# Two decoder layers on one Trainium2 core: the sums of squares of the norms taken for four tiles together in four column groups, and three merge blocks that go through their columns in interleaved runs

## The reference

```
h = rmsnorm(x, g_pre);  proj = h @ w_in
y = mixers(proj)                      # layer 1: S5, short convolution, attention; layer 2: four others
merged = sum_b sigmoid(gate_b) * (y_b @ w_branch_b)     # three branches in layer 1, four in layer 2
x = x + rmsnorm(merged @ w_out, g_post)
x = x + rmsnorm(mlp(rmsnorm(x, g_pre_mlp)), g_post_mlp)
rmsnorm(x, g) = x * rsqrt(mean(x*x over the 1024 channels) + 1e-6) * g
```

## Time and profile before

| | |
|---|---|
| median of three executions | 3498.69 us |
| the profiled execution's own time | 3496.17 us |
| its span, first to last instruction | 3494.5 us (1.7 us lie around it) |
| TensorE busy with matmuls | 3397.4 us, 97% of the span |
| DVE, ScalarE, GpSimd busy | 1357.1, 946.0, 909.0 us |
| mean granted TensorE clock | 0.995 |

### The profile page before, as it was taken

One profiled execution on the slowest core, in us unless ns is written; L12 is line 12 of the kernel. 1 busy time (PEld: TensorE's weight loads), 2 busy tenths in 40 slices (PEclk: granted clock), 3 DMA queues, 4 the chain that ended last, 5 costly groups with the idle time before them and its releaser, 6 DMA issues. The chain is left out here.

```text
span 3494.5 us, 40873 instructions
## 1 busy us (share of the span) xinstructions
PE 3397.4 (97%) x16184; PEld 2791.9 (80%) x16184; DVE 1357.1 (39%) x1651; ACT 946.0 (27%) x1248; POOL 909.0 (26%) x450
## 2 busy tenths in 40 slices
PE   8999999999999999999999999999999999999997
PEld 6788888887877888888868887777778688888886
DVE  6843556444325121212153336554552521121123
ACT  3222434344323111111133333313342411111112
POOL 2211111112341222222422114231254222222225
PEclk9999999999999999999999999999999999999998
DMA  3535434215422111111224323223353211111113
GB/s 128 157 94 157 151 121 151 85 61 211 141 76 79 48 48 48 48 48 48 97 102 132 95 73 127 79 73 141 132 195 124 79 48 48 48 48 48 48 49 131
DMA packets 101602, 333.42 MB, mean 95 GB/s; under 512 B 11920, under 2 KB 21520, under 8 KB 101328
## 3 DMA queue, kind: packets, MB, share of 16 engines
q1 hardware_dynamic: 100432, 327.95, 28.0%
q10 hardware_dynamic: 1040, 3.67, 0.3%
HBM read 249.06 MB, written 85.52 MB: 96 GB/s over the span
## 5 line engine op out<-in xcount | busy, mean ns | idle before, releaser
L282 POOL TENSOR_TENSOR w_lo<-w_raw,w_hi 128x1024 fp32r<-128x1024 f32 (+1 forms) x304 | 698.2, 2301 | 2423.8 <-ACT w_hi L278 2423.7
L322 PE MATMUL pair<-act_hi,w_hi 128*128 128x512 f32 x2976 | 942.8, 398 | 6.6 <-DVE f1v L1957 1.5
L322 PE MATMUL pair<-act_lo,w_hi 128*128 128x512 f32 x2976 | 920.5, 391 | 0.0
L322 PE MATMUL pair<-act_hi,w_lo 128*128 128x512 f32 x2976 | 918.8, 390 | 0.0
L322 PEld LDWEIGHTS pair<-act_hi,w_lo 128*128 128x128 f32 x2976 | 559.3, 188 | 119.6
L322 PEld LDWEIGHTS pair<-act_lo,w_hi 128*128 128x128 f32 x2976 | 559.5, 188 | 119.4
L322 PEld LDWEIGHTS pair<-act_hi,w_hi 128*128 128x128 f32 x2976 | 540.3, 189 | 111.2 <-issue 9.0
L278 ACT CAST w_hi<-w_raw 128x1024 fp32r<-128x1024 f32 x274 | 287.6, 1050 | 866.5 <-PE pair L322 820.7
L609 DVE TENSOR_TENSOR p<-pair,rs 128x1024 f32<-128x1024 f32 x100 | 122.2, 1222 | 402.8 <-PE pair L322 402.7
L1900 DVE TENSOR_TENSOR f2v<-pair,rs 128x1024 f32<-128x1024 f32 x42 | 51.4, 1225 | 333.1 <-PE pair L322 333.1
L322 PE MATMUL pair<-f1hh,w_hi 128*128 128x512 f32 x480 | 147.8, 389 | 0.0
(11 more groups left out here) (478 smaller groups left out, 4065.2 us busy)
## 6 DMA issues: line engine op xcount, KB each, us to landing
w_raw<-in_stream SPq DMA_DIRECT2D x275, 512.0 KB, 3.5
proj<-p SPq DMA_DIRECT2D x101, 512.0 KB, 2.6
m2g<-proj SPq DMA_DIRECT2D x32, 512.0 KB, 4.8
m1g<-proj SPq DMA_DIRECT2D x16, 512.0 KB, 3.4
x<-f1y SPq DMA_DIRECT2D x16, 512.0 KB, 2.6
act_lo<-x SPq DMA_DIRECT2D x16, 512.0 KB, 6.6
foxx<-proj SPq DMA_DIRECT2D x28, 256.0 KB, 5.8
fx_cb<-fox_cum SPq DMA_DIRECT2D x8, 512.0 KB, 7.3
```

The costliest lines, as they stand in the source:

```text
L282: last = nc.gpsimd.tensor_tensor(wlo[:, slot, at:at + n], raw[:, slot, at:at + n], whi[:, slot, at:at + n].bitcast(F32), ALU.subtract)
L322: last = nc.tensor.matmul(out_pair[:, h * HALF:(h + 1) * HALF], wt, a[:, h * HALF:(h + 1) * HALF], start=k == 0 and n_pass == 0, stop=k == ...
```

## The change

In `bridge`, the square of tile k goes to buffer k % 4 of the half row buffers of `late.x`. TensorE no longer sums each square. At k = 3 and k = 7 it waits for the last of four squares and issues four matmuls, each with 32 columns of ones and each into its own 32 partitions of the bank; so group n of partitions holds the sums of tiles n and n + 4. The squares of tiles 4 to 7 wait for the sum at k = 3. Then ScalarE copies the bank to `rs` (`partial`), and `half_sums` of that copy gives, per token on the partitions, 32 times the total; DVE's `half_root` is called without `rows`, so that L472 and L474 go and only the small scale-and-add stays, now after step (1, 1) for half 0. The copy of half 0 stands in ScalarE's queue ahead of everything of half 1; the sum of half 1's copy stands on TensorE ahead of `head.tile(1, 1, 3)`. DVE's first eviction now also waits for the last sum of squares, since the squares lie in `late.x`.

In `products`, blocks 9, 13 and 17 of the first merge address their columns in another order: the 512 columns of a half are taken as two rows of 256, and runs of 32, 64 or 16 columns are taken from the two rows in turn, for the moving operand and for the output alike. The values and where they land are the same.

```diff
@@ -295,7 +295,11 @@
         split_unit(0, 0, 1)
         fetch_unit(2, 0)
-    def products(i, base, per_turn, n_out, tiles, rhs, evict, ahead=False):
+    def in_runs(x, c):
+
+        return x.rearrange("p (a b c) -> p b a c", a=2, c=c) if c else x
+
+    def products(i, base, per_turn, n_out, tiles, rhs, evict, ahead=False, runs=None):
@@ -319,7 +323,8 @@
                 w_hi, w_lo = (x[:, slot, w * P:(w + 1) * P] for x in (whi, wlo))
                 for n_pass, (wt, a) in enumerate(((w_hi, hi), (w_hi, lo), (w_lo, hi))):
                     for h in range(2):
-                        last = nc.tensor.matmul(out_pair[:, h * HALF:(h + 1) * HALF], wt, a[:, h * HALF:(h + 1) * HALF],
+                        half, c = slice(h * HALF, (h + 1) * HALF), runs[o] if runs and o in runs else None
+                        last = nc.tensor.matmul(in_runs(out_pair[:, half], c), wt, in_runs(a[:, half], c),
                                                 start=k == 0 and n_pass == 0, stop=k == tiles - 1 and n_pass == 2)
                 if w == 7 or (not packed and k == tiles - 1):
                     last.then_inc(s_mm, 1)
@@ -331,13 +336,13 @@
                 yield
             evict(i, o, out_pair, ready, reads.mark)
-    def stage(turns, per_turn, n_out, tiles, rhs, evict, per=None, ahead=False):
+    def stage(turns, per_turn, n_out, tiles, rhs, evict, per=None, ahead=False, runs=None):
         if ahead:
             b = used["units"] + 1
             split_unit(b, b % 2, b // 2 + 1)
         if turns == 1:
-            for _ in products(0, used["units"], per_turn, n_out, tiles, rhs, evict):
+            for _ in products(0, used["units"], per_turn, n_out, tiles, rhs, evict, False, runs):
                 pass
         else:
             assert per_turn % 2 == 0 and n_out % 2 == 0
@@ -545,14 +550,16 @@
             split[h, k] = V.mark(V.after(a).scalar_tensor_tensor(act_lo[:, k, half], yk, g,
                                                                  act_hi[:, k, half].bitcast(F32),
                                                                  ALU.mult, ALU.subtract))
-            free = (done[h][k - 2],) if k > 1 else (done[0][-1], summed) if h else ()
-            a = A.mark(A.after(*free).activation(sq(h, k % 2), yk, ACT.Square))
+            a = A.mark(A.after(done[h][-1] if k > 3 else done[0][-1] if h else None).activation(sq(k % 4), yk, ACT.Square))
             PE.after(split[h, k])
             head.tile(0, h, k)
             if k >= lag[h]:
                 head.tile(1, h, k - lag[h])
-            PE.after(a)
-            done[h].append(PE.mark(nc.tensor.matmul(sides[h], ones[:], sq(h, k % 2), start=k == 0, stop=k == KT - 1)))
+            if k % 4 == 3:
+                PE.after(a)
+                for n in range(4):
+                    last = nc.tensor.matmul(sides[h][32 * n:32 * n + 32, :], ones[:, 0:32], sq(n), start=k == 3, stop=k == KT - 1)
+                done[h].append(PE.mark(last))
         add(0, 0)
         for k in range(KT):
@@ -568,23 +575,29 @@
             if k == 5:
                 y_scale[1] = half_spread(1, bank[1][:], root)
         if next_gain:
+            partial = A.mark(A.after(done[0][-1]).copy(rs[:, halves[0]], sides[0]))
             for k in range(KT - lag[0], KT):
                 head.tile(1, 0, k)
         add(1, 0)
         for k in range(KT):
             step(1, k)
             if next_gain and k == 0:
-                root = half_root(2, sides[0], 1.0 / D, done[0][-1], rs[:, halves[0]])
+                total = half_sums(sides[0], rs[:, halves[0]], True, True, partial)
+            if next_gain and k == 1:
+                root = half_root(2, sides[0], 1.0 / (32 * D), total)
             if next_gain and k == 2:
                 spread = half_spread(2, sides[0], root)
             if next_gain and k == 3:
                 rs_ready = A.mark(A.after(spread).copy(rs[:, halves[0]], sides[0]))
         if next_gain:
+            partial = A.mark(A.after(done[1][-1]).copy(rs[:, halves[1]], sides[1]))
             for k in range(KT - lag[1], KT):
+                if k == 3:
+                    total = half_sums(sides[1], rs[:, halves[1]], True, True, partial)
                 head.tile(1, 1, k)
-            V.after(rs_ready)
+            V.after(rs_ready, done[1][-1])
             head.evicted(0, 0, head_evict)
-            root = half_root(3, sides[1], 1.0 / D, done[1][-1], rs[:, halves[1]])
+            root = half_root(3, sides[1], 1.0 / (32 * D), total)
             head.evicted(1, 0, head_evict)
             spread = half_spread(3, sides[1], root)
             V.after(A.mark(A.after(spread).copy(rs[:, halves[1]], sides[1])))
@@ -1804,7 +1817,7 @@
             fetch_gate(o, *stored[o])
         yield
         open_gate(0)
-        stage(1, n_out * tiles // 8, n_out, tiles, rhs, evict)
+        stage(1, n_out * tiles // 8, n_out, tiles, rhs, evict, runs={9: 32, 13: 64, 17: 16} if branches == 3 else None)
         barrier()
         yield
@@ -1820,8 +1833,8 @@
             self.hh, self.hl = sb(at, name + "hh", [P, 8, L], F32R), sb(at, name + "hl", [P, 8, L], F32R)
             self.x = sb(at, name + "v", [P, 2, L])
-        def square_row(self, h, n):
-            return (self.x[:, 0, 0:HALF], self.x[:, 0, HALF:L], self.sq[:, 0:HALF])[h + n]
+        def square_row(self, n):
+            return self.x[:, n // 2, n % 2 * HALF:(n % 2 + 1) * HALF]
     def mix_out(late, x_dram, gain, out_dram, next_gain, head_evict):
```

## The result

The changed kernel takes 3505.22 us (median of 16 runs, 3499.41 to 3508.18), the kernel before 3497.05 in the same session (16 runs, 3494.45 to 3501.35). The ratio is 1.0021, 95% interval 1.0014 to 1.0029: slower by some 7 us. The profiled execution took 3504.86 us, its span is 3503.2. The forecast was 3494.5 and no measurable difference. Among the kernels of the experiments two executions, one of 6351.85 us and one of 10398.28, ran at mean clocks of 0.80 and 0.32; they are left out of the ratios and of the times at the low clock.

What follows compares the result with a forecast made beforehand. TensorE's matmuls bound the kernel, with DVE carrying the norm stretches' second half. Stretches -5.1, ends +0.35, runs +0.6 make -4.2 on 3496.2, so 3492.0; the median, 2.5 above, was forecast at 3494.5 us, range 3488 to 3508.

Steps and rivals of the forecast that it cites:

- The batch: Four gathered sums of squares on TensorE in the norm stretches: 1.2 us, against 3.4 for four single sums.
- the cases with less overlap: A batch whose column groups overlap less: 2.05 us gives 3505, 2.5 gives 3510, no overlap (3.4 + 0.36) gives 3525.
- rival 1: Batches overlap less in every norm stretch; each 0.1 us more costs 1.2 in all; chance 0.16, half beyond +7.
- the 2.5: Batch time if matmuls start and end strictly in program order: five turns of 0.427 plus the changes, giving 3510.
- the prediction's sign of being right: In the trace, the batch's records (L555's successors) start 7 ns apart in fours; next matmul 1.2 us after a batch.
- The steps of half 0: First stretch: L477 0.85 us earlier without the sum ahead of it; L529 of half 1 starts 1.25 earlier.
- The wait for `act_hi(1, 0)`: DVE waits 2.2 us ahead of half 1's first split, as ScalarE copies the bank before `act_hi(1, 0)`.
- That for tile 5's: Half 0: tile 4's square waits for the batch with tile 5's `act_hi` behind; split ends about 1052.3, little earlier.
- The ends: Last split to next stage: 10.9 us; -0.9 first stretch, +0.45 second, +0.8 third, together +0.35.
- The runs: Merge blocks 9, 13 and 17: 0.98 ns a gap, at most 1.3 us; taken as +0.6.
- rival 3: TensorE's granted clock around the norm stretches: -1.5 to +4.5 us, taken as 0; with fast batches about 3489, chance 0.14.
- The sentence on half 1: TensorE has 0.69 us of work in 2.05 there; a clock fall costs nothing while DVE leads, up to 1.5 otherwise.

Runs made afterwards that it cites:

- the two kernels shown above: Batched sums without merge runs, two unused matmuls added per half: in TensorE's waits, 3496.9 us; behind squares 0 and 1 with ScalarE's queue reordered, 3492.5 us.
- the order of the queue: Against batched sums without merge runs (3502.7 us): tile 4's square and the partial copy each moved behind the next `act_hi` on ScalarE; 3496.9 us.
- both together: Batched sums without merge runs, plus unused matmuls and ScalarE's reordered queue: three in half 0 3494.0, three in both halves 3494.4, two behind squares 0 and 1 3492.5 us.
- the fourth: Batched sums without merge runs, ScalarE's queue reordered, one unused matmul in steps 0 and 1 of both halves, between add and split; 3497.8 us.
- The order kernel: Batched sums without merge runs, tile 4's square and the partial copy moved behind the next `act_hi` on ScalarE, no added matmuls; 3496.9 us, ratio 1.0002.
- one kernel: Batched sums without merge runs, two unused matmuls added in each half where TensorE waits, ScalarE's queue as in the change; 3496.9 us, ratio 1.0007.
- these two kernels: Batched sums without merge runs, reordered ScalarE queue, two unused matmuls per half: behind squares 0 and 1, 3492.5 us; between add and split, 3497.8 us.

## Why the prediction was wrong, by its own steps

- **The batch**: taken as 1.2 us, measured 1.00 at full clock and up to 1.26 where it began at 0.50. The bounds of the cases with less overlap, 2.05 and more, are out; rival 1 fell. The Trainium skill, page "TensorE: Matmul & The Clock Gate", section on packing small matmuls, says that matmuls start and end in program order, and the prediction made 2.5 of that: the trace doesn't agree with the 2.5. The records of a batch start in two groups of four, some 7 ns apart at full clock, as the prediction's sign of being right says. Whether the rule itself is broken isn't shown, since the 2.5 also supposed that the two records of one matmul follow each other directly.
- **The steps of half 0**: L477 was to be 0.85 earlier. At full clock it is (the wait is 2.21 before, 1.38 and 1.36 in the two kernels shown above). In the changed kernel it is 4.18. The step was right in its arithmetic and wrong in the duration: it took times of rows at 1.00 for a piece that ran at 0.50. Half 0 as a whole was to be 1.25 shorter, 21.9, and is 22.0 in the one piece at full clock; in the changed kernel it is 26.2, 23.3 and 26.3.
- **The wait for `act_hi(1, 0)`**: taken as 2.2 us, measured 1.89, and in the sum. Half 1 was to be 0.45 shorter, 19.5, and is 18.8 at full clock. That for tile 5's, which the prediction had as a new wait with the split "little earlier than before", is 0.22 at full clock and 1.63 behind a batch at the low one.
- **The ends**: the first eviction was to wait for the batch, and does, 2.14 us. In the changed kernel the ends stayed at 1.00 and take 11.0 us each, where the prediction had 10.9, 10.9 and some 12.0: 0.3 less than before in all, forecast +0.35. The third was mis-sized by 1. In other executions 3 us at 0.50 reached into an end and made it 12.4 to 12.6.
- **The runs**: taken as 0.6, measured 0.24 + 0 + 0.32 and 0.05 behind it. Right in the sum. Not right in its form: 0.98 ns a gap would be 8, 16 and 31 ns a matmul for runs of 64, 32 and 16, and it was 0, 10 and 13. The sentence of the Trainium skill, page "PSUM — Partial Sum Buffer", specifications, that any non-contiguous output slows matmuls significantly is not borne out: 6% at worst, nothing at runs of 64. The other section of the Trainium skill that the prediction set against it ("Advanced Engine Details and Errata", PSUM cachelines) has the same sentence beside the one on two elements, so the two don't differ as it said.
- **The clock** is the step that failed. The prediction had it as rival 3, "I take 0", with bounds of -1.5 to +4.5, "in half 1 TensorE now has 0.69 of work in 2.05", and "a fall there costs nothing while DVE leads". It asked where TensorE would be idlest and stopped at half 1. It didn't ask it of half 0, where the first three sums were also the work that filled TensorE's waits ahead of its longest piece, in which it leads; with three matmuls put back there the time at 0.50 in the stretches is 27 us and not 48. The clock fell in both halves of all three stretches, and the low time of an execution is 82 us for 40. The sentence on half 1 is wrong as well: 6.8 us at 0.50 there make it 20.5 to 20.7 us where the same text takes 18.8. Part of how TensorE's low clock is paid on VectorE's chain is seen in the waits: a late batch holds the next `act_hi` back in ScalarE's queue, 1.63 us for 0.22. Only the gain of rival 3 came true: behind the first stretch the clock stayed up, 1.4 us.

How the 7 us come about: the sums should have given 4.75 us in the stretches and cost 5.8 in all. By the estimate above they would have given 7.2 at full clock, more than forecast, and the falls of the clock took 15.0 in the profiled execution. Matmuls added against the low clock take back 4.8 to 5.8 us by the medians (3.5 to 4.9 by the ratios), since they cost time of their own; the order of the queue takes back 5.8 (5.2), and both together 8.2 to 10.8 in three kernels (the last from the two ratios, 1.0017 and 0.9986) and 4.9 in the fourth. The order kernel (3496.9 at 71 us) doesn't show a second cause beside the clock: some 3.6 us of its gain are there at full clock too, mostly from a wait that the prediction had priced. Only the rest, by the same traces some 2 us, is a price of the low clock that is paid through ScalarE's queue.

The range (3488 to 3508) held the time; it did so with the batch's bounds, for another reason than the one that came true. That was luck: the clock's own bound was +4.5 us.

Open: what decides whether an emptied piece is followed by a low one, since one kernel kept its clock behind 0.98 in 3.40. With it stays open why one place of the same two matmuls kept the clock better than the other (46 and 56 us); the 5 us between these two kernels go with their falls.

## What to carry to other kernels

Work on an engine that waits anyway is not free to remove when it is what keeps TensorE's clock up: before a sum is taken out, read the busy time of the pieces between the waits ahead of the next stretch in which TensorE leads, and price that stretch at the clock of 0.50 as one of the cases. When several small operations are gathered into one late one, look on every in-order queue at what stands behind the first instruction that waits for it, and put the next urgent operation ahead; but don't take a gain from that as proof that the wait was the loss. Two quick tests of the clock are to add unused matmuls and see whether the kernel gets faster, and to compare pieces of the same text that ran at different clocks.

## What the runs showed of the hardware that I had not expected

- Unused matmuls, 7.7 us of them, made the kernel 4.9 us faster (3502.7 to 3497.8).
- A piece of the same text took 18.8 us at full clock, 20.1 with 3.6 us at 0.50 and 20.7 with 6.8, although VectorE leads in it.
- Eight float32 records of 512 columns, four sums in four column groups, took 1.00 us at full clock, where one such sum of full width, two records, takes 0.85.
- A matmul of 512 columns that reads and writes in runs of 64 costs nothing more, in runs of 32 10 ns (5.68 against 5.44 us for 24) and in runs of 16 13 ns (5.76). The step from 16 to 32 gaps costs 3 ns, that from 8 to 16 costs 10.
- The executions of before themselves scatter with the clock: of 33, the fastest (3489.1 us) had a mean clock of 0.997, the slowest (3499.3) 0.993.
